# Raw residual times norm gain as matmul operand, late inverse roots, and token-stationary matmuls for the second expert table, in a fused two-block transformer kernel

## The reference, cut to what matters

```python
def rmsnorm(x, g):
    y = x * rsqrt(mean(x * x, axis=-1) + EPS)
    return y * g

def sq_relu_mlp(h, w_up, w_down):              # w_up 1024 x 4096, w_down 4096 x 1024
    return square(relu(h @ w_up)) @ w_down

x = x + dsa_mixer(...)                          # ends in o @ w_o
x = x + sq_relu_mlp(rmsnorm(x, g_mlp[0]), w_up[0], w_down[0])
hs = rmsnorm(x, g_kv);  kv = hs @ w_kv          # 1024 x 1536, then compress_blocks
x = x + nsa_mixer(rmsnorm(x, g_attn[1]), ...)   # ends in o @ w_o
x = x + sq_relu_mlp(rmsnorm(x, g_mlp[1]), w_up[1], w_down[1])

# experts: a = gelu(h @ u_tab.T) at the chosen experts, w = gate * a
out = einsum('te,ted->td', w, v_tab[experts])   # computed here as a dense product with all of v_tab
x = x + gate2 * out
```

## Time and profile before

| | |
|---|---|
| Median of 3 runs | 1942.89 us (1941.92 to 1943.19) |
| Profiled execution: its time, its span | 1943.62 us, 1942.0 us |
| Mean granted TensorE clock | 0.922 |
| Busy: PE, DVE, ACT, POOL | 1718.2, 1049.7, 856.5, 427.0 us |
| Second expert table, 128 slots | about 369 us |
| Each MLP, 64 slots | about 187 us |

### The profile page before, as it was taken

How to read it: one execution, slowest core, us unless ns; L and a number is a source line. 1 busy time by engine, 2 the same in 40 slices (tenths; PEclk the granted TensorE clock), 3 DMA queues, 4 the chain that set the end, 5 groups by cost and what they waited for, 6 DMA issues and landing times.

```text
span 1942.0 us, 37247 instructions
## 1 busy us (share of the span) xinstructions
PE 1718.2 (88%) x12944; PEld 1623.6 (84%) x12944; DVE 1049.7 (54%) x2365; ACT 856.5 (44%) x1782; POOL 427.0 (22%) x369
## 2 busy tenths in 40 slices
PE   3785879999999999999999977578999698879997
PEld 1574669999999999999999966478999667679996
DVE  4546548944777732555555532745554514645554
ACT  2213335564444444555555531435555313546653
POOL 2010347986666676000000010000000000000000
PEclk9885689999999999999999987698999797989998
DMA  8472124554444445555555531023555272035552
GB/s 291 168 272 88 55 95 145 174 176 135 139 136 139 140 163 183 180 181 182 183 184 183 183 112 65 22 98 132 182 184 184 87 238 87 10 105 180 182 184 98
DMA packets 80749, 287.59 MB, mean 148 GB/s; under 512 B 10080, under 2 KB 11408, under 8 KB 80432
## 3 DMA queue, kind: packets, MB, share of 16 engines
q1 hardware_dynamic: 70416, 256.93, 39.6%
q0 software_dynamic: 7344, 26.35, 3.8%
q10 hardware_dynamic: 2928, 3.52, 0.5%
HBM read 284.14 MB, written 2.62 MB: 148 GB/s over the span
## 4 chain that ended last, share of the span: by engine, by line
PE 82%; DVE 9%; ACT 3%; issue 2%; DMA 2%; POOL 1%; ACTq 1%; POOLq 0%; DVEq 0%; SPq 0%
PE pu L467 12%; PE pu L468 12%; PE pu L469 12%; PE pacc L467 10%; PE pacc L468 9%; PE pacc L469 9%; PE pu L439 3%; PE pn L457 2%; PE pacc L524 2%; PE pu L449 2%; PE pn L679 1%; PE pm L679 1%; DVE big L1247 1%; POOL ring_lo L322 1%; DMA big<-in_ada 1%
## 5 line engine op out<-in xcount | busy, mean ns | idle before, releaser
L315 ACT ACTIVATE ring_hi<-ring 128x512 fp32r<-128x512 f32 x880 | 506.9, 624 | 639.3 <-PE pu L469 372.5
L467 PE MATMUL pu<-Xh,ring_hi 128*128 128x256 f32 x1984 | 578.4, 292 | 41.7 <-DVE Xl L1235 16.6
L322 DVE TENSOR_TENSOR ring_lo<-ring,ring_hi 128x512 fp32r<-128x512 f32 x592 | 382.3, 689 | 362.4 <-ACT ring_hi L315 362.3
L468 PE MATMUL pu<-Xl,ring_hi 128*128 128x256 f32 x1984 | 569.6, 287 | 0.0
L469 PE MATMUL pu<-Xh,ring_lo 128*128 128x256 f32 x1984 | 569.3, 287 | 0.0
L467 PEld LDWEIGHTS pu<-Xh,ring_hi 128*128 128x128 f32 x1984 | 389.4, 196 | 46.0 <-issue 31.5
L322 POOL TENSOR_TENSOR ring_lo<-ring,ring_hi 128x512 fp32r<-128x512 f32 x288 | 370.4, 1308 | 148.1 <-ACT ring_hi L315 143.4
L468 PEld LDWEIGHTS pu<-Xl,ring_hi 128*128 128x128 f32 x1984 | 389.7, 196 | 0.0
L469 PEld LDWEIGHTS pu<-Xh,ring_lo 128*128 128x128 f32 x1984 | 389.0, 196 | 0.0
L467 PE MATMUL pacc<-vh,ring_hi 128*128 128x256 f32 x1024 | 290.0, 283 | 0.0
L468 PE MATMUL pacc<-vl,ring_hi 128*128 128x256 f32 x1024 | 289.8, 283 | 0.0
(11 more groups left out here) (277 smaller groups left out, 1949.5 us busy)
## 6 DMA issues: line engine op xcount, KB each, us to landing
ring<-in_weights SPq DMA_DIRECT2D x488, 512.0 KB, 3.2
big<-in_ada POOLq DMA_DIRECT2D x48, 512.0 KB, 5.8
bias_row<-big ACTq DMA_DIRECT2D x1, 1536.0 KB, 13.5
XT<-in_xT ACTq DMA_DIRECT2D x1, 1024.0 KB, 10.7
big<-bias_row POOLq DMA_DIRECT2D x8, 128.0 KB, 2.4
outT<-sq SPq DMA_DIRECT2D x1, 1024.0 KB, 3.9
big<-in_c ACTq DMA_DIRECT2D x1, 512.0 KB, 5.6
big<-in_keys ACTq DMA_DIRECT2D x1, 128.0 KB, 8.3
```

The source lines that it names most:

```text
L315: nc.scalar.activation(ring_hi[:, n % 2, half], ring[:, n % RING, half], ACT.Copy).then_inc(s["split_hi"], 1)
L322: api.tensor_tensor(ring_lo[:, n % RING, half], ring[:, n % RING, half], ring_hi[:, n % 2, half], ALU.subtract).then_inc(s[LOW[name][0]], 1)
L467: mm(out, ring_hi[:, n % 2, w], xh, start=start, stop=False, skip_group_check=True)
L468: mm(out, ring_hi[:, n % 2, w], xl, start=False, stop=False, skip_group_check=True)
```

## The change

1. **MLP starts.** `residual` becomes `raw_residual` on VectorE and `after_product` on ScalarE. As soon as chunk i of `XT` is complete, ScalarE writes the high part of `XT` times the norm's gain (`raw_high`) and the square of the chunk (`raw_square`), and VectorE the low part (`raw_low`). The inverse root isn't in it. TensorE's first MLP slot (`raw_slot`) waits for the parts chunk by chunk. GpSimd adds the eight squares (`add_squares`), and a single matmul with ones (`one_sum`) sums over the partitions. The inverse root is applied when a PSUM tile is evacuated: VectorE's `relu` computes max(tile, 0) times the inverse root. ScalarE then squares twice, into `act_t` and into the high part.
2. **Keys and values.** VectorE adds the MLP's result chunk by chunk, the raw parts follow, and TensorE sums the squares between the chunks of its first slot (`sum_chunk`). VectorE evacuates all twelve products, eight of them times the inverse root (`kv_out`), and makes `HS` and `HTb` between them; the four token products wait for all of `HS`. The windows come behind the twelfth evacuation on VectorE.
3. **Second expert table.** `token_slot` holds 128 experts x 128 tokens stationary and moves 512 columns of the weights: 12 matmuls to a slot. `pacc` then holds tokens on partitions. After the stage ScalarE and VectorE copy one half each to SBUF, `turn_back` transposes it in 16 steps, and VectorE adds the result to `XT`.

```diff
@@ tensor
+            def raw_slot(name, between):
+                n, (xh, xl) = SLOT[name], raw_x[name]
+                pe.wait_ge(s["evacs"], USE[name] - 1)
+                for c in range(C):
+                    if c % 4 == 0:
+                        split_ready(name, 0, c // 4, None)
+                    pe.wait_ge(s["raw_lo"], RAW[name] + c + 1)
+                    last = three(entry(USE[name]), n, slice(c * P, (c + 1) * P), xh[:, c, :], xl[:, c, :], c == 0, c == C - 1)
+                    between(c)
+                last.then_inc(s["slots_used"], 1)
+            def token_slot(name, k, xh, xl, g):
+                n = SLOT[name] + k
+                for half, w in enumerate(halves):
+                    split_ready(name, k, half, g)
+                    for tt in range(TT):
+                        out = paccf[:, tt * D + half * 512:tt * D + (half + 1) * 512]
+                        rows = slice(tt * P, (tt + 1) * P)
+                        mm(out, xh[:, rows], ring_hi[:, n % 2, w], start=False, stop=False, skip_group_check=True)
+                        mm(out, xl[:, rows], ring_hi[:, n % 2, w], start=False, stop=False, skip_group_check=True)
+                        last = mm(out, xh[:, rows], ring_lo[:, n % RING, w], start=False, stop=False, skip_group_check=True)
+                last.then_inc(s["slots_used"], 1)
+            def turn_back(count):
+                pe.wait_ge(s["acc_copied"], 2 * count)
+                for c in range(C):
+                    for tt in range(TT):
+                        last = nc.tensor.transpose(turned_acc(c)[:, tt * P:(tt + 1) * P],
+                                                   scr[:, tt * D + c * P:tt * D + (c + 1) * P], ident[:, :])
+                    if c % 2:
+                        last.then_inc(s["turned"], 1)
...
-                    down_slot("peer_v", k, vh[:, k % 2, :], vl[:, k % 2, :], g)
+                    token_slot("peer_v", k, vh[:, k % 2, :], vl[:, k % 2, :], g)
             close_acc()
+            turn_back(1)
...
             def mlp(name):
-                norm_sum(NORM[name])
-                pe.wait_ge(s["normed"], NORM[name])
                 open_acc()
+                raw_slot(name, lambda c: None)
+                one_sum(name)
+                for k in range(1, 4):
+                    up_slot(name, k, USE[name] + k, None, 4, None, raw_x[name])
+                four_down(None)
...
-            norm_sum(NORM["attn1"])
-            pe.wait_ge(s["hs_ready"], 1)
-            for i in range(8):
-                up_slot("kv", i, USE["kv"] + i, None, 0, "kv" if i == 0 else None)
+            raw_slot("kv", lambda c: sum_chunk("kv", c - 1, False) if c else None)
+            sum_chunk("kv", C - 1, True)
+            for i in range(1, 8):
+                up_slot("kv", i, USE["kv"] + i, None, 0)
+            pe.wait_ge(s["hs_ready"], C)
@@ scalar
+            def after_product(product, name):
+                for i in range(C):
+                    act.wait_ge(s["evacs"], USE[product] + i + 1)
+                    raw_high(name, i)
+                    raw_square(name, i)
+                    if i + 2 < C:
+                        split_high(act, product, i + 2)
+                    else:
+                        split_high(act, name, i + 2 - C)
...
                 def hidden_tile(k, g=None):
-                    act.wait_ge(s["slots_used"], tick(g, BODY, SLOT[name] + k + 1))
-                    f(relu_t[:, j, :], entry(USE[name] + j), ACT.Relu).then_inc(s["evacs"], 1)
                     act.wait_ge(s["evacs"], tick(g, 4, USE[name] + done + 1))
-                    f(act_t[:, j, :], relu_t[:, j, :], ACT.Square).then_inc(s["act_f32"], 1)
-                    act.wait_ge(s["act_f32"], tick(g, 4, tiles + done + 1))
-                    f(act_h[:, j, :], act_t[:, j, :], ACT.Copy).then_inc(s["act_hi"], 1)
+                    f(act_t[:, j, :], relu_t[:, j, :], ACT.Square)
+                    f(act_h[:, j, :], relu_t[:, j, :], ACT.Square).then_inc(s["act_hi"], 1)
@@ vector
+            def raw_residual(product, name):
+                for i in range(C):
+                    e = USE[product] + i
+                    dve.wait_ge(s["slots_used"], SLOT[product] + i + 1)
+                    v.tensor_tensor(XT[:, i, :], entry(e), XT[:, i, :], ALU.add).then_inc(s["evacs"], 1)
+                    if i:
+                        raw_low(name, i - 1)
+                    if i + 2 < C:
+                        split_low(dve, v, product, i + 2)
+                    elif i + 2 == C:
+                        split_low(dve, v, name, 0)
+                raw_low(name, C - 1)
+                split_low(dve, v, name, 1)
...
+                def relu(k, g=None):
+                    j, done = k % 4, (k // BODY) * 4 + k % 4
+                    dve.wait_ge(s["slots_used"], tick(g, BODY, SLOT[name] + k + 1))
+                    v.scalar_tensor_tensor(relu_t[:, j, :], entry(USE[name] + j), 0.0, R[:, 0:T], ALU.max, ALU.mult)\
+                        .then_inc(s["evacs"], 1)
...
                         split_low(dve, v, name, j + 2, g)
                         if j < 4:
-                            hidden_low(j, g)
+                            relu(j, g)
+                        if 1 <= j < 5:
+                            hidden_low(j - 1, g)
...
+            for i in range(8):
+                if i + 2 < 8:
+                    split_low(dve, v, "kv", i + 2)
+                kv_out(i)
+                v.scalar_tensor_tensor(HS[:, i, :], XT[:, i, :], column("kv_sh", i), R[:, 0:T], ALU.mult, ALU.mult)\
+                    .then_inc(s["hs_ready"], 1)
+                last = v.scalar_tensor_tensor(HTb[:, i, :], XT[:, i, :], column("attn", C + i), R[:, 0:T], ALU.mult, ALU.mult)
             last.then_inc(s["normed"], 1)
-            for i in range(4, 8):
-                split_low(dve, v, "kv", i)
+            for i in range(8, 12):
+                kv_out(i)
             v.memset(hx, 0.0)
```

More of the change, by code:

```diff
@@ L72 @@
         _n[_sem] += _k
-XSPLIT = {n: i for i, n in enumerate(["w_out", "peer", "a_o", "mlp0", "kv", "b_in", "b_o", "mlp1"])}
+XSPLIT = {n: i for i, n in enumerate(["w_out", "peer", "a_o", "b_in", "b_o"])}
+RAW = {n: C * i for i, n in enumerate(["mlp0", "kv", "mlp1"])}
 KV_TILES = (0, 1, 2, 3, 4, 5, 8, 9, 6, 7, 10, 11)
@@ L89 @@
 NORM = {n: i + 1 for i, n in enumerate(NORMS)}
+SQUARED = {n: i + 1 for i, n in enumerate(n for n in NORMS if n not in ("mlp0", "attn1", "mlp1"))}
 def attention_units():
@@ L410, in _, with add_squares @@
                                     pattern=[[0, NH], [-1, T]], channel_multiplier=1).then_inc(s["bias_ready"], 1)
+            def add_squares(name):
+                for c in range(1, C):
+                    pool.wait_ge(s["raw_sq"], RAW[name] + c + 1)
+                    last = nc.gpsimd.tensor_tensor(ssum, sq[:, 0, :] if c == 1 else ssum, sq[:, c, :], ALU.add)
+                    if c < C - 1:
+                        step(last)
+                last.then_inc(s["sum_ready"], 1)
             pool.wait_ge(s["bias_ready"], 1)
@@ L479, in up_slot, with one_sum, sum_chunk @@
                             pe.wait_ge(s["x_split"], 2 * XSPLIT[x] + c // 4 + 1)
-                    last = three(entry(e), n, slice(c * P, (c + 1) * P), Xh[:, c, :], Xl[:, c, :], c == 0, c == C - 1)
+                    last = three(entry(e), n, slice(c * P, (c + 1) * P), xs[0][:, c, :], xs[1][:, c, :], c == 0, c == C - 1)
                 last.then_inc(s["slots_used"], 1)
+            def raw_slot(name, between):
[8 more added lines that the diff above has]
+                last.then_inc(s["slots_used"], 1)
+            def one_sum(name):
+                pe.wait_ge(s["sum_ready"], ("mlp0", "mlp1").index(name) + 1)
+                mm(pn[:, 0:T], ones[:, :], ssum, start=True, stop=True).then_inc(s["sums"], 1)
+            def sum_chunk(name, c, last_one):
+                pe.wait_ge(s["raw_sq"], RAW[name] + c + 1)
+                last = mm(pn[:, 0:T], ones[:, :], sq[:, c, :], start=(c == 0), stop=(c == C - 1), skip_group_check=True)
+                if last_one:
+                    last.then_inc(s["sums"], 1)
             def down_slot(name, k, xh, xl, g):
@@ L1170, in mlp @@
                         hidden_tile(k)
+            after_product("a_o", "mlp0")
             mlp("mlp0", 4, 0)
             split_high(act, "kv", 0)
-            act.wait_ge(s["x_ready"], 5)
-            squares(XT[:, :, :], sq[:, :, :])
-            root(NORM["attn1"])
-            split_high(act, "kv", 1)
-            act.wait_ge(s["hs_ready"], 1)
-            both_high(HS)
-            for i in range(12):
-                if i + 2 < 8:
-                    split_high(act, "kv", i + 2)
-                evac(SLOT["kv"] + i, KV[:, KV_TILES[i], :], entry(USE["kv"] + i))
+            for c in range(C):
+                act.wait_ge(s["x_chunks"], c + 1)
+                raw_high("kv", c)
+                raw_square("kv", c)
+            split_high(act, "kv", 1)
+            root(NORM["attn1"])
```

(20 more changed lines are left out.)

104 lines of the change are left out of this document (61 added, 43 removed).

## The result

The changed kernel takes 1887.97 us (median of 4 runs, 1885.30 to 1888.26); the kernel before took 1942.41 us in the same session (4 runs, 1941.34 to 1943.19). The ratio is 0.9718, 95% interval 0.9705 to 0.973. It is 54.4 us faster, where 74.8 were forecast.

What follows compares the result with a forecast made beforehand. TensorE, holding 82% of the chain, was taken as the bound, through its matmul time and its waits for norms. Terms summed to -74.8 us from 1943.6, giving 1868.8 and a median of 1868.1 us; range 1857 to 1906.

Steps and rivals of the forecast that it cites:

- its own sign: Stated test of failure: second-table matmul pitch outside 213 to 227 ns, or `relu` late by over 0.5 us a round.
- Second table: Second expert table: 512-column matmuls at 216.7 ns, half the instructions, slot 2.60 us instead of 2.88; -35.8 us.
- Turning back: Behind the second expert table: two copies side by side, 16 transposes and adds, hidden by nothing; +2.1 us.
- MLPs, starts and rounds: Two MLP starts no longer wait for the norm, -34.2 us; longer ScalarE/VectorE chains in 16 rounds, +3.2.
- Rings of `a_o`, `b_o`: Loops of `a_o` and `b_o`: add, raw high, square and splits form one ring, 3.0 us against 2.88; +1.4 us.
- Keys and values: Key/value part: 15.9 us gained to the token products, 4.4 lost waiting for the windows; -11.5 us.
- Rival (a): Second table: 13 ns belong to each instruction, pitch 226.7 ns; +15.4, 1883.5 us; chance 0.17.
- (b): Second table: the limit is per column, pitch 240 ns, nothing gained there; +35.8, 1903.9 us; chance 0.11.
- (e): Second table: 512-column form streams at two cycles a column, 427 ns; slower, +323, 2191 us; chance 0.03.
- (f): Norms: relocated sums still end ahead of every product, only the table gains; 1909.2 us; chance 0.03.
- Rival (d): MLPs: chains keep TensorE longer, 1 us a round and 5 a start; +22.8, 1890.9 us; chance 0.05.
- Rival (c): Clock falls in new short waits, at three restarts and the raw key/value slot; +12.5, 1880.6 us; chance 0.07.

Runs made afterwards that it cites:

- e1: Changed kernel plus blocks of independent matmuls on TensorE behind all its work, other engines idle; run once for its trace: fp32r 512 columns took 227.3 ns.
- e8: Changed kernel plus further matmul blocks behind its work (other widths, stationary operands, data types); run once for its trace: fp32r 384 columns took 173.9 ns.
- e2: Changed kernel, but the second expert table's matmuls move 256 columns instead of 512, activations still stationary; 1905.40 us.
- e6: Changed kernel, but TensorE sums the eight squares itself at each MLP start and GpSimd adds nothing; 1888.92 us.
- e4: Changed kernel, but ScalarE evacuates key/value products 8 to 11, so VectorE makes the windows under the token products; 1878.66 us.
- e5: Changed kernel, but in the `a_o` and `b_o` loops ScalarE splits weights before the raw parts, except for the last chunk; 1887.84 us.
- e11: e10 plus zero-matrix matmuls at the four other places where e9 has them, with 80 instead of 56 in one; 1869.72 us.
- e10: e7 plus 11 idle matmuls of a zero matrix in the wait ahead of the first key/value slot; 1876.26 us.
- after: The changed kernel itself, without any follow-up edit, against the kernel before; 1887.97 us.
- e7: Changed kernel with the edits of e4 and e5 together: windows early and weight split first in `a_o` and `b_o`; 1879.77 us.
- e9: e4 plus idle matmuls of a zero matrix, which nobody reads, in five waits of TensorE; 1874.58 us.

## Why the prediction came out as it did

The direction held, and so did what was said of the norms; the largest term was mis-sized. By its own sign the prediction was wrong, for the pitch of the table, 228.9 ns, lies outside 213 to 227. All values are changes of the profiled execution in us, taken between starts on TensorE.

| Step | Forecast | Measured |
|---|---|---|
| Second table | -35.8 | -16.9 |
| Turning back | +2.1 | +2.0 |
| MLPs, starts and rounds | -34.2 + 3.2 | -35.1 |
| Rings of `a_o`, `b_o` | +1.4 | +4.3 |
| Keys and values, with the first 64 compression products | -11.5 | -8.7 |
| The rest | 0 | -1.0 |
| Sum | -74.8 | -55.4 |

The smaller terms miss by 4.1 and 1.0 us one way and by 2.9 and 2.8 the other; that they nearly cancel is luck.

**The second table: the term that failed, 18.9 of the 19.4 us.** The step is "I take 216.7, 0.5 under that nearest row". It read the cost above streaming off f32 records and concluded that an array busy for 512 cycles hides all but 4 ns. e1 and e8 show that the surcharge of an fp32r matmul with 128 stationary columns is 13 to 14 ns at 256, 384 and 512 columns alike, with nothing beside it. Rival (a), 226.7 ns, is what happened (227.3 alone, 228.9 in the stage), and its 1883.5 us is 4.5 from the median. The argument against it, the f32 records, came from another kind of operation; the one fp32r row at hand, 13.3 ns at 256 columns, was the nearer one. Rivals (b) and (e) asked for 240 and 427 ns, and (f) for late norms; the windows exclude all three. The prediction counts (f) among those that are not faster; at its 1909.2 us it would be faster too. That turning the operands round is itself worth nothing (e2) was assumed and is now shown.

**Turning back.** The copy took 1.23 us and the adds started 0.70 behind the first transpose; from `close_acc` to the squares 6.3 us pass, against 4.35 before.

**The MLPs: right, a little better than forecast.** The start was read right to two tenths: one wait of 1.5 us ahead of the third slot where 1.7 was written (the matmuls around it start 1.63 apart), clock 1.00 throughout, no wait for a chunk. What was wrong was the 0.2 us per round. The distance between two `split_high`s with a tile between them is

```profile
1315.37 1.14 ACT L326 ACTIVATE ring_hi<-ring 128x512 fp32r<-128x512 f32 x2
...
1318.31 1.14 ACT L326 ACTIVATE ring_hi<-ring 128x512 fp32r<-128x512 f32 x2
```

2.94 us, where 3.25 had been summed from the lengths of records. The squares' records are 0.42 and 0.40 us long, but the next instruction starts 0.32 behind the first and 0.31 behind the second. Over the few tiles of a round TensorE never felt it. Rival (d) falls with this. GpSimd's cover was priced too low: without it (e6) a start loses 3.0 us, and not 1, since fourteen more records of about 0.22 us stand in the chain.

**The rings: right mechanism, too small.** 3.22 us to a slot instead of 3.0 (whose own numbers give 1.7 for fourteen slots, not 1.4). `a_o` became 1.7 us longer, and so did `b_o` where its clock is full (e4); the other 0.95 of the 4.3 is the clock at the start of `b_o`, which took 1.5 us before and 2.4 after. Of the 3.22, 0.19 is GpSimd's doing (e6 without it: 3.03); GpSimd's addition had been booked as hidden, which it is from TensorE but not from VectorE. e5 shows that the order of two instructions on ScalarE is worth the whole of it locally.

**Keys and values: -15.5 to the token products, as forecast (15.9), and the wait for the windows 4.14 us, as forecast (4.4).** What was missing is its echo: the clock fell in that wait and the first 64 compression products cost 2.8 us more than at the full clock. Rival (c) had the lowered clock, but in the raw slots, and not here. e4 takes both away.

## What to carry to other kernels

Price an instruction form from rows of the same data type: a surcharge per instruction seen at one width stays at another until a row shows otherwise, and then halving the number of instructions gives back about half of it. A chain on an in-order engine is priced by start-to-start distances, not by record lengths, and a helper on GpSimd is not free while VectorE works on two SBUF operands. For each wait that a change leaves on TensorE, add as a bound what the products behind it cost at half clock: after one and the same wait of 2.81 us the eleven traces lost 0, 1.5 or about 2.5 us. For the same reason read differences of 2 us between two kernels from several executions, not from one trace. Where the wait can't be closed, matmuls of a zero matrix inside it can keep the clock: with four more blocks of them e11 is 6.5 us under e10.

## What the runs showed of the hardware that was not expected

- An fp32r matmul at full clock costs 13 to 14 ns above streaming at 256, 384 and 512 columns with 128 stationary columns; bf16 costs 2.7 at 128 and 256, and an f32 record 2.5 at 256 columns. At 128 moving and 128 stationary columns it takes 110.8 ns, where bf16 takes 56.0.
- VectorE is slowed by GpSimd: the split pair from 1.29 to 1.48 us beside an addition of 0.74, the scaling of eight chunks from 3.25 to 4.58 beside a mask of 1.95.
- A wait of 4.1 us was followed by about 6 us at the half clock (1521.3 to 1527, at 0.50), which cost 2.8 us; one of 2.81 us ahead of `b_o` by 1.00 in four traces and by the half clock for up to 6 us in seven; one of 1.7 us ahead of the first key/value slot was followed by a clock of 1.00 in after and e4, and of 0.58 in e5 and e7, which split first in `a_o` and `b_o`. What decides stays open. With eleven matmuls of zeros (1.36 us) in that last wait it was 1.00 in all three traces, which doesn't show that they were the reason.
- Matmuls of zeros in five waits raised the mean granted clock from 0.935 to 0.943, and in e11 no other stretch was seen to pay for it: sums that took 5.2 to 6.7 us in the kernels without them took 3.72.
